# The second block's recurrence with tokens on the partitions, values with a column of ones streamed, and eight transposes a head

## The reference

```python
scores = jnp.einsum('bhcld,bhcsd->bhcls', qc, kc) * d
num = jnp.einsum('bhcls,bhcsd->bhcld', scores, vc) + inter_scale[..., None] * num_inter
den = jnp.sum(scores, axis=-1) + inter_scale * den_inter
h = num / jnp.maximum(jnp.abs(den), jnp.exp(-m_t))[..., None]
...
hb = h_fwd + h_bwd
hb = hb * lax.rsqrt(jnp.mean(hb * hb, axis=-1, keepdims=True) + EPS)
hb = hb.transpose(0, 2, 1, 3).reshape(B, S, D_MLSTM) * mlstm_norm_g.astype(jnp.float32)
y_b = hb.astype(x.dtype) * jax.nn.sigmoid(o) * jax.nn.silu(z_b)
```

## Time and profile before

| what | us |
|---|---|
| median of 3 runs | 1835.36 (1834.73 to 1837.48) |
| the profiled execution, whole | 1838.12 |
| its span, first to last instruction | 1836.3 |
| TensorE busy in the span | 1742.6 (95%) |
| VectorE, ScalarE, GpSimd busy | 686.1, 684.5, 671.1 (37% each) |
| mean granted TensorE clock | 0.971 |

### The profile page before, as it was taken

One profiled execution on the slowest core, in us unless ns is written; L12 is line 12 of the kernel. 1 busy time (PEld: TensorE's weight loads), 2 busy tenths in 40 slices (PEclk: granted clock), 3 DMA queues, 4 the chain that ended last, 5 costly groups with the idle time before them and its releaser, 6 DMA issues.

```text
span 1836.3 us, 23357 instructions
## 1 busy us (share of the span) xinstructions
PE 1742.6 (95%) x8464; PEld 1430.0 (78%) x8464; DVE 686.1 (37%) x1054; ACT 684.5 (37%) x960; POOL 671.1 (37%) x295
## 2 busy tenths in 40 slices
PE   6999999999999999999999978989898889999997
PEld 5888888878886677888888867778787778877876
DVE  2222220124127623322220048465757452372323
ACT  4443432235346634444331234424242423234431
POOL 4444444443340034444444433322222223444443
PEclk9999999999999899999999979899999999999998
DMA  3222222242220012222222212111111111322221
GB/s 141 101 93 94 100 91 103 92 137 93 80 81 13 1 56 71 92 103 91 100 94 94 101 46 81 69 58 57 57 57 57 46 58 69 115 91 92 96 96 71
DMA packets 41523, 148.73 MB, mean 81 GB/s; under 512 B 4608, under 2 KB 4608, under 8 KB 41216
## 3 DMA queue, kind: packets, MB, share of 16 engines
q1 hardware_dynamic: 39968, 141.58, 22.2%
q10 hardware_dynamic: 1504, 6.45, 1.1%
HBM read 144.86 MB, written 2.10 MB: 80 GB/s over the span
## 4 chain that ended last, share of the span: by engine, by line
PE 64%; issue 25%; POOL 5%; DVE 3%; ACT 1%; DMA 0%; POOLq 0%; DVEq 0%; SPq 0%; ACTq 0%
PE ps L469 15%; PE ps L470 14%; PE ps L471 14%; POOL w_lo L408 5%; PE ps L539 4%; PE ps L541 4%; PE ps L540 4%; PE ps L477 2%; PE ps L713 1%; PE ps L703 1%; PE ps L691 1%; PE ps L484 1%; DVE scr L1459 1%; DMA x<-in_x 0%; ACT h_hi L1067 0%
## 5 line engine op out<-in xcount | busy, mean ns | idle before, releaser
L408 POOL TENSOR_TENSOR w_lo<-w_raw,w_hi 128x1024 fp32r<-128x1024 f32 x262 | 633.2, 2417 | 995.3 <-ACT w_hi L1047 995.3
L1047 ACT ACTIVATE w_hi<-w_raw 128x1024 fp32r<-128x1024 f32 x260 | 275.5, 1060 | 950.4 <-PE ps L471 758.0
L469 PE MATMUL ps<-h_hi,w_hi 128*128 128x512 f32 x1504 | 599.7, 399 | 19.9 <-DVE h_lo L1455 9.3
L470 PE MATMUL ps<-h_lo,w_hi 128*128 128x512 f32 x1504 | 593.2, 394 | 0.0
L471 PE MATMUL ps<-h_hi,w_lo 128*128 128x512 f32 x1504 | 592.7, 394 | 0.0
L469 PEld LDWEIGHTS ps<-h_hi,w_hi 128*128 128x128 f32 x1504 | 287.5, 191 | 87.3 <-issue 15.9
L471 PEld LDWEIGHTS ps<-h_hi,w_lo 128*128 128x128 f32 x1504 | 286.8, 191 | 61.1
L470 PEld LDWEIGHTS ps<-h_lo,w_hi 128*128 128x128 f32 x1504 | 287.6, 191 | 58.0
L1469 DVE TENSOR_TENSOR hid<-silu,ps 128x512 f32<-128x512 f32 x44 | 30.3, 688 | 305.6 <-PE ps L471 305.6
L539 PE MATMUL ps<-hid_hi,w_hi 128*128 (+1 forms) x352 | 137.2, 390 | 0.0
L541 PE MATMUL ps<-hid_hi,w_lo 128*128 (+1 forms) x352 | 137.0, 389 | 0.0
(11 more groups left out here) (284 smaller groups left out, 1805.0 us busy)
## 6 DMA issues: line engine op xcount, KB each, us to landing
w_raw<-in_units SPq DMA_DIRECT2D x262, 512.0 KB, 3.2
x<-in_x SPq DMA_DIRECT2D x4, 512.0 KB, 8.0
w<-in_w ACTq DMA_DIRECT2D x1, 2048.0 KB, 7.8
out<-x SPq DMA_DIRECT2D x8, 256.0 KB, 2.0
scr<-proj ACTq DMA_DIRECT2D x8, 128.0 KB, 4.5
inv_count<-in_inv_count ACTq DMA_DIRECT2D x1, 1024.0 KB, 4.8
const<-in_const ACTq DMA_DIRECT2D x1, 899.0 KB, 7.4
q_sc<-in_row_const ACTq DMA_DIRECT2D x1, 512.0 KB, 3.5
```

What stands on the lines that cost most here:

```text
L408: nc.gpsimd.tensor_tensor(w_lo[:, slot, :], w_raw[:, slot, :], w_hi[:, slot, :].bitcast(F32), ALU.subtract).then_inc(w_lo_done, 1)
L469: nc.tensor.matmul(ps[:, bank, :], whi, hi[:, k, :], start=(n == 0), stop=False)
L470: nc.tensor.matmul(ps[:, bank, :], whi, lo[:, k, :], start=False, stop=False)
L1047: nc.scalar.activation(w_hi[:, slot, :], w_raw[:, slot, :], ACT.Copy).then_inc(w_hi_done, 1)
```

## The change

The numerator gets tokens on its partitions. The stationary operand is now `d_mat` or `q_sc` (128 tokens), and the values and the state are streamed, as rows of 257: 256 values and one column of ones. So the denominator is one number a token, the floor of it comes as a column per chunk (`floor_tok`, turned once ahead of the heads, in place of a row spread in each head), and the result `h_tok` has tokens on the partitions too. ScalarE squares it chunk by chunk and sums along the row, the root needs no spreading, VectorE scales each chunk by it, and eight transposes turn the result back to channels, into banks 2 and 3, behind unit 9. Two operations then apply the norm's gain and the gates and write `yb`. The state's addition streams 257 columns too. The keys of the next head, which go into the same banks 2 and 3, wait for `y_done` of the head before. Its core:

```diff
+VW = MD + 1
+Y_FREE = 2
...
                 def turn_keys_values():
-                    pe.wait_ge(hrms_done, p + 1)
+                    pe.wait_ge(y_done, Y_FREE + 2 * p)
                     pe.wait_ge(qk_done, 4 * p + 4)
...
-                    if d:
-                        pe.wait_ge(fl_done, 2 * p + 1)
-                    nc.tensor.matmul(ps[:, 3, :], sel[:, d, :], row_f[:, :], start=True, stop=True).then_inc(fl_ready, 1)
...
-                            mm = nc.tensor.matmul(ps[:, 4 + e, 0:MD + P], k_w[:, d, e * P:(e + 1) * P], v_aug[:, c, :],
+                            mm = nc.tensor.matmul(ps[:, 4 + e, 0:VW], k_w[:, d, e * P:(e + 1) * P], v_aug[:, c, :],
                                                   start=True, stop=True)
...
-                    for e in range(3):
-                        o = ps[:, 6 + d, e * P:(e + 1) * P]
-                        mm = nc.tensor.matmul(o, v_aug[:, c, e * P:(e + 1) * P], d_mat[:, d, at], start=(e == 0),
-                                              stop=False, skip_group_check=True)
-                        for f in range(2 if s else 0):
-                            mm = nc.tensor.matmul(o, c_state[:, d, f, e * P:(e + 1) * P], q_sc[:, d, f, at],
-                                                  start=False, stop=False, skip_group_check=True)
+                    o = ps[:, 6 + d, 0:VW]
+                    mm = nc.tensor.matmul(o, d_mat[:, d, at], v_aug[:, c, :], start=True, stop=(s == 0))
+                    for f in range(2 if s else 0):
+                        mm = nc.tensor.matmul(o, q_sc[:, d, f, at], c_state[:, d, f, :], start=False, stop=(f == 1))
                     mm.then_inc(num_ready, 1)
...
+                def turn_outputs():
+
+                    for c in range(NCH):
+                        pe.wait_ge(hn_tok_done, NCH * p + c + 1)
+                        for e in range(2):
+                            mm = nc.tensor.transpose(ps[:, 2 + e, c * MC:(c + 1) * MC], h_tok[:, c, e * P:(e + 1) * P], ident)
+                    mm.then_inc(y_turned, 1)
...
-                    for e in range(2):
-                        nc.scalar.activation(d_mat[:, e, :], h_sum[:, e, :], ACT.Square).then_inc(hsq_done, 1)
+                    for c in range(NCH):
+                        nc.scalar.activation(sq_junk[:, c, :], h_tok[:, c, :], ACT.Square, accum_out=ssq[:, c:c + 1]
+                                             ).then_inc(hsq_done, 1)
...
-                    chain.link(nc.vector.scalar_tensor_tensor(den[:, d, :], q_n, -1.0, floor[:, d, at], ALU.mult, ALU.max))
-                    chain.link(nc.vector.tensor_tensor(den[:, d, :], den[:, d, :], q_n, ALU.max))
-                    chain.link(nc.vector.reciprocal(den[:, d, :], den[:, d, :]))
...
+                    chain.link(nc.vector.tensor_scalar(den[:, d:d + 1], q_n, lowest, None, ALU.max))
+                    chain.link(nc.vector.scalar_tensor_tensor(den[:, d:d + 1], q_n, -1.0, den[:, d:d + 1], ALU.mult, ALU.max))
+                    chain.link(nc.vector.reciprocal(den[:, d:d + 1], den[:, d:d + 1]))
...
                     nc.vector.reciprocal(r_col[:, :], r_col[:, :]).then_inc(hrstd_done, 1)
+                    dve.wait_ge(hrstd_done, p + 1)
+                    for c in range(NCH):
+                        nc.vector.tensor_scalar(h_tok[:, c, :], h_tok[:, c, :], r_col[:, c:c + 1], None, ALU.mult
+                                                ).then_inc(hn_tok_done, 1)
...
-                        y, og = h_sum[:, e, :], merged[:, bass.ds(2 * p + e, 1), :].rearrange("p a t -> p (a t)")
-                        chain.link(nc.vector.scalar_tensor_tensor(y, y, p_("g_mlstm")[:, bass.ds(2 * p + e, 1)],
-                                                                  ps[:, 7, :], ALU.mult, ALU.mult))
-                        nc.vector.tensor_tensor(y, y, og, ALU.mult).then_inc(y_done, 1)
+                        og = merged[:, bass.ds(2 * p + e, 1), :].rearrange("p a t -> p (a t)")
+                        nc.vector.scalar_tensor_tensor(yb[:, e, :], ps[:, 2 + e, :], p_("g_mlstm")[:, bass.ds(2 * p + e, 1)],
+                                                       og, ALU.mult, ALU.mult).then_inc(y_done, 1)
```

More of the change, by code:

```diff
@@ L215, in build @@
         k_tok = sb("k_tok", [P, NCH, MD], F32, heads)
-        v_aug = sb("v_aug", [P, NCH, MD + P], F32, heads)
+        v_aug = sb("v_aug", [P, NCH, VW], F32, heads)
         d_mat = sb("d_mat", [P, 2, T], F32, heads)
@@ L230, in build @@
         wk_tok = sb("wk_tok", [P, NCH, 64], F32, heads)
+        floor_tok = sb("floor_tok", [P, NCH, 64], F32, heads)
         keep_bc = sb("keep_bc", [P, 2 * MH * NCH], F32, heads)
@@ L840, in turn_rows @@
                 pe.wait_ge(row_exp, 1)
-                for n, (src, bank) in enumerate(((rows_of[3][0:64], 5), (rows_of[2][0:64], 6))):
+                for n, (src, bank) in enumerate(((rows_of[3][0:64], 5), (rows_of[2][0:64], 6), (raw_f, 4))):
                     for c in range(NCH):
@@ L958, in mlstm @@
                 if core and units:
-                    spread_roots()
+                    turn_outputs()
             def merge_b():
@@ L1000, in pooled @@
                     mm.then_inc(unit_done, 1)
-                pe.wait_ge(y_done, DC + 4)
+                pe.wait_ge(y_done, Y_FREE + DC + 4)
             def output():
@@ L1339, in mlstm @@
                         if i == 6:
-                            act.wait_ge(y_done, 2 * MH)
+                            act.wait_ge(y_done, Y_FREE + 2 * MH)
                         nc.scalar.activation(merged[:, i, :], ps[:, i % 2, :], ACT.Sigmoid,
@@ L1389, in pooled @@
                     for c in range(4 * n, 4 * n + 4):
-                        act.wait_ge(y_done, 2 * MH + c + 1)
+                        act.wait_ge(y_done, Y_FREE + 2 * MH + c + 1)
                         nc.scalar.activation(y_hi[:, c, :], scr[:, c, :], ACT.Copy).then_inc(y_hi_done, 1)
@@ L1740, in row_columns @@
                 dve.wait_ge(row_exp, 1)
-                for row, raw in ((row_m, raw_m), (row_i, raw_i), (row_f, raw_f)):
+                for row, raw in ((row_m, raw_m), (row_i, raw_i)):
                     nc.vector.tensor_tensor(row[64:P, :], raw, row[0:64, :].bitcast(F32), ALU.subtract)
-                for n, dst in enumerate((a_tok, wk_tok)):
+                for n, (dst, bank) in enumerate(((a_tok, 5), (wk_tok, 6), (floor_tok, 4))):
                     dve.wait_ge(tokrow_ready, n + 1)
-                    nc.vector.tensor_copy(dst[:, :, :].rearrange("p c r -> p (c r)"), ps[:, 5 + n, 0:NCH * 64])
-                dve.wait_ge(tokrow_ready, 3)
+                    nc.vector.tensor_copy(dst[:, :, :].rearrange("p c r -> p (c r)"), ps[:, bank, 0:NCH * 64])
+                dve.wait_ge(tokrow_ready, 4)
                 nc.vector.tensor_copy(keep_bc[:, :], ps[:, 7, 0:2 * MH * NCH]).then_inc(tokrow_done, 1)
@@ L1826, in step @@
                         for e in range(2):
-                            new, add = c_state[:, d, e, :], ps[:, 4 + e, 0:MD + P]
+                            new, add = c_state[:, d, e, :], ps[:, 4 + e, 0:VW]
                             if s == 0:
@@ L1976, in _ @@
                 dve.sem_inc(credit, 2)
+            dve.sem_inc(y_done, Y_FREE)
             dve.sem_inc(hid_done, 2)
```

68 lines of the change are left out of this document (26 added, 42 removed).

## The result

| what | before | after |
|---|---|---|
| median, first comparison | 1836.07 us | 1807.29 us (1803.77 to 1817.45, 4 runs) |
| median, second comparison | 1838.47 us | 1805.86 us (1799.92 to 1809.64, 5 runs) |
| the profiled execution, span | 1836.3 us | 1802.0 us |
| mean granted TensorE clock | 0.971 | 0.972 |

The ratio is 0.985, with a 95% interval of 0.983 to 0.987; in the second comparison, on the chip that the first experiments shared, 0.982 (0.980 to 0.985). The change takes 29 to 33 us off; 24 were forecast, and the time lies inside the forecast's range. It is faster, and by more than was worked out.

What follows compares the result with a forecast made beforehand. TensorE, busy 95% of the span, bounds the kernel. Heads 1 to 3 gain 22.1 us, two boundaries lose 11.0, the last head gains 15.4: 26.5, less 2.7 for head 3's clock, leaves 24: 1811 us, range 1801 to 1822.

Steps and rivals of the forecast that it cites:

- Heads: Time from the keys of head 1 to the first merge pass, 363.2 us before; forecast to lose 24.2.
- The pass of 257 columns: TensorE in steps: 0.217 us a pass, on a straight line between 128 columns (0.107) and 384 (0.32).
- Rival C: TensorE passes of 257 columns cost more than their columns; slower from 0.10 above 0.217, up to 1861 us; chance 0.05.
- Steps 2 and 3: In each head, step 2's key weighting gets in ahead of GpSimd's w_lo; 8.33 becomes 5.64 us, gain 2.7.
- Rival A: Key weighting comes behind w_lo after all, at steps 2 and 3 and early in the last head: 1818 us; chance 0.17.
- Steps 0 and 1: Heads 1 to 3: step 1 still waits for VectorE's state copy; shorter copies and step 1 gain 0.8 us.
- the extra fall of the clock in head 3: Behind step 1's stall, lengthened to 4 us, the clock falls in head 3 too; 2.7 us lost.
- The boundary: Behind heads 1 and 2: squares gain 1.7, transposes lose 0.1, y_done wait 4.8, clock 2.3; -5.5 us each.
- B: Clock does not fall at the boundaries, nor in head 3: 9.6 us less, 1801.4 us; chance 0.12.
- D: No change, 1835 us: boundary waits cost 8 us more each, scaled chunks or y_done coming later; chance 0.03.
- The clock's price: Behind each boundary's idle 4.7 us, TensorE runs 4.6 us at half clock, 2.3 us lost.
- The last head: Gains 15.4 us in sum; the new y_done wait replaces the 5.88 us wait for the keys' copy.

Runs made afterwards that it cites:

- second profile: Profile of the changed kernel measured again unaltered, as yardstick for the experiments: 1805.86 us, ratio 0.982 of the kernel before; heads 331.6 us.
- the wide kernel: Changed kernel with 128 columns of ones in place of one (width 384, orientation kept): 1838.07 us, 0.9996 of the kernel before.
- late weighting: Changed kernel with one more VectorE wait, so step 2's key weighting starts only when step 2's numerator is done: 1814.59 us.

## Why the prediction was right, point by point

"Heads" was forecast to lose 24.2 us (24, and the 0.3 of the four transposes, which lie ahead of them), and lost 28.9, and 31.6 in the second profile. By stretches as in the windows above the forecast was 4.2, 1.9, -0.8 and 18.9 (each boundary's wait with the head ahead of it, its clock with the head behind); measured 4.7, 2.4, 2.3 and 19.5.

- **The pass of 257 columns.** 10 passes 2.17 forecast; measured 1.98, and 0.11 more in the unit behind, 2.09. Steps 4 and 5 gained 2.26 for 2.1, steps 6 and 7 1.52 for 1.3. The straight line held; the wide kernel confirms it from the other side. Rival C is out.
- **Steps 2 and 3.** 2.7 forecast, 2.78 measured, less 0.1 in the unit behind. The weighting was 0.17 ahead (0.16 forecast). Rival A did not happen; made to happen, it cost 5.0 us in waits for the 5.2 that were said of these steps, and as much again in falls of the clock, 8.7 by the median. Its 2.2 for steps 0 and 1 of the last head were not tried.
- **Steps 0 and 1.** 0.8 forecast, 0.9 measured in head 1 with the unit behind. The stall stayed, 4.2 in place of 3.67, and the extra fall of the clock in head 3 came. The prediction laid it to the longer stall, but the kernel before with nothing but the new wait has it too, at 3.67; so it is not the length of the stall alone that brought it. Moving the convolutions shows that VectorE's order is its cause.
- **The boundary.** Keys 5.70 behind unit 9 forecast, 5.68 measured. Squares 1.71 forecast and measured. The three waits are 4.45, 4.45 and 4.37, "near 4.7" was said; the clock fell at all three. Rivals B and D are out.
- **Where the forecast was 4.7 us short.** The clock's price. The 2.3 us a boundary were added to a stretch that was not free of waits before. The earlier trace rows end ahead of this row of the kernel before, TensorE at the first spread row of head 2, which I had not read:

```profile
1276.20 0.50 PE L897 MATMUL ps<-row_m,sel 128*128 128x512 f32 x1 [0.43 <-DVE k_tok L1791]
```

The keys' copy stands on VectorE behind the y products, so in heads 2 and 3 it was late already: from the keys to that row 9.60 and 9.58 before, where head 1 takes 9.00. The new wait takes this one's place, as in the last head, where I did count it. So the boundary's half clock cost 1.85 and 1.15 net, not 2.3 twice: 1.6 us. The extra fall in head 3 cost 1.7, not 2.7: 1.0. The two make up 2.6 of the 4.7 by which the forecast was short; the rest is spread over the four stretches, 0.1 to 0.9 each, and which operations it lies in was not followed up. In the second profile the forecast is 7.4 short; there the stall in head 2 is 1.0 shorter, and the stalls cost about 1.2 less at the half clock.
- **The last head.** 18.9 forecast, 19.5 measured: no wait for the keys' copy, step 1 waits 1.01 where it waited 2.83, and 0.78 at step 6 where it waited 1.72. Its weighting at step 0 came 0.06 ahead of `w_lo` and took 0.35; the forecast put it first without a row that says so, and that it was first is luck.

So the mechanism held, and the term that was sized worst is the price of the boundary, taken too high because the rows behind the keys were not read for the wait that the new one would replace.

The version with other banks and moved convolutions is 3.5% faster than the kernel before, 1.7% faster than the changed one.

## What to carry to other kernels

A denominator that comes as a block of identical columns costs its full width in each matmul; one column is enough once tokens lie on the partitions, and here it is the width that paid: turned round at the full width, the kernel took the same time as before. When outputs are turned back through banks that the next iteration needs first, look for banks that it needs last: here that choice was worth 17 us, over half of what the change itself brought. And a stall that survives a change is worth a look at the order of the engine that it waits for: VectorE's list had five operations standing ahead of the one that TensorE needed.

## What the runs showed of the hardware

- The order of two operations 0.1 us apart decides. The weighting 0.17 ahead of `w_lo` took 0.35 (and `w_lo` 2.39), and still 0.35 when only 0.06 ahead (`w_lo` 2.50, last head of the changed kernel); 0.10 behind its start it took 2.39 (last head of the kernel before), 0.21 to 0.26 behind 2.24 to 2.28, 0.84 behind 1.65, 1.13 behind 1.36. When behind, it ended 0.15 after `w_lo` each time. The Trainium skill, SBUF — State Buffer, section Who interferes with whom, says that the one that issues first has the shared ports for its whole instruction and the other blocks fully; these rows agree. A copy out of PSUM, 0.17 behind, took 0.76, its usual time; that section says that an instruction with at most one SBUF input, outside the modes that take both port pairs, does not contend, and the row agrees. The weighting has one such input as well; by that section it must run in one of these modes, which no trace here shows.
- The granted clock behind an idle stretch of TensorE, at the steps, the boundaries and the scores of all fourteen profiles: behind 4.1 us and more it fell every time; behind 3.7 to 3.8 eight times of nine (not in head 3 of the kernel before); behind 2.8 never, in eight cases; but behind 2.4 to 2.6 eight times of nine (step 3 with the late weighting, three of four; step 1 of the last head with 384 columns, 0.78; the scores ahead of the last head, four of four); behind 1.8 and less never. 3.7 us of passes with no use kept it up. A length of idle time alone does not tell it.
- ScalarE's square with a sum along the row is recorded as two operations, 0.40 and 0.18 us for 256 columns; four chunks took 1.7 us under unit 8 and cost TensorE nothing.
